# A chunked delta rule: chunk sums over halves of 64 tokens instead of 128 tokens

## The reference, cut to what matters

```python
def step(S, inp):
    r_t, w_t, k_t, v_t, kk_t, a_t = inp
    s_kk = jnp.einsum('bhij,bhj->bhi', S, kk_t)
    S = S * w_t[:, :, None, :] - s_kk[..., None] * (kk_t * a_t)[:, :, None, :] + v_t[..., None] * k_t[:, :, None, :]
    return S, jnp.einsum('bhij,bhj->bhi', S, r_t)
```

## Time and profile before

| | |
|---|---|
| time, median of 3 runs | 2954.65 us (2952.22 to 2955.24) |
| time of the profiled execution | 2943.12 us |
| its span | 2941.3 us |
| mean granted TensorE clock | 0.961 of 2.4 GHz |
| PE busy in the span | 2727.4 us (93%) |
| DVE busy | 991.0 us (34%) |
| ACT busy | 622.2 us (21%) |

### The profile page before, as it was taken

How to read it: one execution, slowest core, us unless ns; L and a number is a source line. 1 busy time by engine, 2 the same in 40 slices (tenths; PEclk the granted TensorE clock), 3 DMA queues, 4 the chain that set the end, 5 groups by cost and what they waited for, 6 DMA issues and landing times. The chain is left out here.

```text
span 2941.3 us, 35988 instructions
## 1 busy us (share of the span) xinstructions
PE 2727.4 (93%) x15314; PEld 1573.6 (53%) x15314; DVE 991.0 (34%) x2175; ACT 622.2 (21%) x1297; POOL 63.4 (2%) x61
## 2 busy tenths in 40 slices
PE   8998879899999989899679999999798986999998
PEld 7776645588874456574333333333585743444443
DVE  3513445223330238385611111111573752111212
ACT  4222215211110111272401000000313621000102
POOL 0000000000000000000001111111000000000000
PEclk9999979999999999999889999999898998999999
DMA  4137671122222031100369999999120027999995
GB/s 156 65 116 284 231 312 37 72 72 79 79 86 88 0 141 44 43 2 29 143 248 371 385 384 387 381 390 392 52 72 29 16 104 295 404 422 422 422 422 238
DMA packets 87476, 582.00 MB, mean 198 GB/s; under 512 B 10186, under 2 KB 11754, under 8 KB 21780
## 3 DMA queue, kind: packets, MB, share of 16 engines
q1 hardware_dynamic: 78244, 554.66, 47.9%
q0 software_dynamic: 6544, 21.24, 2.5%
q10 hardware_dynamic: 2528, 3.80, 0.3%
HBM read 561.96 MB, written 17.70 MB: 197 GB/s over the span
## 5 line engine op out<-in xcount | busy, mean ns | idle before, releaser
L1998 PE MATMUL ps<-both,ring 128*128 128x257 f32 x1408 | 308.6, 381 | 1.6 <-PEq L1628 1.6
L2911 PE MATMUL ps<-ring,xsL 128*64 128x512 f32 x1320 | 297.5, 602 | 5.7 <-ACTq L217 5.7
L1998 PEld LDWEIGHTS ps<-both,ring 128*128 128x128 f32 x1408 | 268.2, 191 | 42.0 <-issue 1.9
L2911 PEld LDWEIGHTS ps<-ring,xsL 128*64 128x64 f32 x1320 | 100.7, 139 | 193.7 <-issue 187.7
L3142 DVE TENSOR_TENSOR hidL<-hidL,ps 128x1024 f32<-128x1024 f32 x16 | 19.5, 1222 | 463.7 <-PE ps L2911 463.7
L1816 PE MATMUL ps<-ring,actT 128*128 128x512 f32 x352 | 153.6, 598 | 6.9 <-PEq L1986 6.9
L2510 PE MATMUL ps<-both,ring 128*128 128x384 f32 x480 | 157.5, 490 | 1.9 <-PEq L1809 1.9
L2911 PE MATMUL ps<-ring,htL 128*64 128x512 f32 x640 | 145.2, 605 | 3.4 <-ACTq L217 3.2
L856 PE MATMUL ps<-both,ring 128*128 128x264 f32 x640 | 143.8, 386 | 1.5 <-PEq L633 1.5
L3172 ACT ACTIVATE hidL<-ps 128x1024 f32<-128x1024 f32 x16 | 16.4, 1024 | 555.2 <-PE ps L2919 318.5
L856 PEld LDWEIGHTS ps<-both,ring 128*128 128x128 f32 x640 | 121.4, 190 | 23.0 <-issue 2.4
(11 more groups left out here) (536 smaller groups left out, 3671.6 us busy)
## 6 DMA issues: line engine op xcount, KB each, us to landing
ring<-in_w_exp SPq DMA_DIRECT2D x245, 1024.0 KB, 12.9
ring<-in_w SPq DMA_DIRECT2D x73, 1024.0 KB, 5.1
tokens_b<-in_w_exp SPq DMA_DIRECT2D x63, 1024.0 KB, 12.4
ring<-in_w_mod SPq DMA_DIRECT2D x48, 1024.0 KB, 5.2
h<-in_w_exp SPq DMA_DIRECT2D x37, 1024.0 KB, 17.1
lent<-in_w_exp SPq DMA_DIRECT2D x26, 1024.0 KB, 15.5
both<-in_w_exp SPq DMA_DIRECT2D x13, 1024.0 KB, 18.1
gb<-in_rows SPq DMA_DIRECT2D x8, 512.0 KB
```

The lines of the kernel that those rows point to most:

```text
L1998: mm = pe.matmul(k.ps[:, 4 * (j % 2) + 2 * gv + h, 0:HALF], w(c_), hT[:, c_, FIRST + h * HALF:FIRST + (h + 1) * HALF], start=c_ == 0, stop ...
L2911: mm = pe.matmul(ps[HD * par:HD * par + HD, bank + half, :], lhsL(kk, par), weights(kk)[:, half, par, :], start=kk == 0, stop=kk == KD - 1 ...
```

## The change

In step 10 the contraction is cut in two. The 128 tokens are taken as two halves (r = 0, 1) of 64 tokens; each half is contracted by itself, with 4 chunks x 64 = 256 moving columns, and goes to a PSUM bank of its own (bank + r), with g now choosing the left or right 256 columns of it. So there are 24 matmuls with a 64 x 64 stationary operand and 256 columns, in place of 12 with 128 x 64 and 512. They are also issued in another order: the two p and the two r of one product follow each other.

Since the halves are apart, one mask of four columns serves both: `side` is 1 where the token's chunk number modulo 4 is the column. So `ex` has four copies of each kind in place of eight: DVE makes four in step 9 in place of eight, ACT eight in `expand` in place of sixteen.

The diagonal of decays is written to `aT` by `keep_decay`, which DVE runs after it has announced step 9 (`steps.tell(moved.sem)`), and no longer in step 10. In step 10 DVE first waits for its own earlier instructions (`steps.join()`), then does the two subtractions. Reads of PSUM in step 10 now span two banks each.

For the tile of 16 tokens there is one half and one mask column, so its matmuls are the same 12 in another order.

```diff
--- before.py
+++ after.py
@@ -101,7 +101,7 @@
     parts["mask_u"] = np.concatenate([-1.0 * upper, 1.0 * upper], 1)
     parts["mask_o"] = np.concatenate([-1.0 * upper_in, 1.0 * upper_in], 1)
     parts["mask_l"] = -1.0 * lower
-    parts["chunk_of"] = (p[:, None] // CH == np.arange(CPT)[None, :])
+    parts["side"] = (p[:, None] // CH % 4 == np.arange(4)[None, :])
     parts["eye_head"] = (p[:, None] % HD == np.arange(HD)[None, :])
     parts["scan_keep"] = np.broadcast_to(np.arange(T1) % CH != 0, (P, T1))
     first_only = len(parts)
@@ -1167,8 +1167,9 @@
     tkn = sb("tok", [P, 4, RW])
     w = sb("tk", [P, 3, RW])
     spare = k.stream.ring[:, RING // 2:RING, :].rearrange("p s c -> p (s c)")
-    n_ex, n_a = 3 * CPT * RW, 2 * 2 * CPT * HD
-    ex = spare[:, 0:n_ex].rearrange("p (a c h) -> p a c h", a=3, c=CPT)
+    n_ex, n_a = 3 * 4 * RW, 2 * 2 * CPT * HD
+    ex = spare[:, 0:n_ex].rearrange("p (a c h) -> p a c h", a=3, c=4)
+    FOUR = 4 * CH
     aT = spare[:, n_ex:n_ex + n_a].rearrange("p (n g c j) -> p n g c j", n=2, g=2, c=CPT)
     gT = sb("gT", [P, 2, 2, P])
     hT_ = sb("hT_", [P, 2, 2, P])
@@ -1183,6 +1184,7 @@
     def steps_of(t):
         n, it = ns[t], t % 2
         nc_ = n // CH
+        groups, sides = -(-n // FOUR), min(nc_, 4)
         ts = slice(P * t, P * t + n)
 
         def hp(x, g, p):
@@ -1293,34 +1295,43 @@
 
         def dv9(dve):
             return [dve.tensor_tensor(gT[:, it, :, 0:n], both_g(0), rho[:, :, ts], ALU.add)] + [
-                dve.tensor_scalar(ex[0:n, 2, ch, :], w[0:n, 1, :], c("chunk_of")[0:n, ch:ch + 1], -1.0, ALU.mult, ALU.mult)
-                for ch in range(nc_)]
+                dve.tensor_scalar(ex[0:n, 2, x, :], w[0:n, 1, :], c("side")[0:n, x:x + 1], -1.0, ALU.mult, ALU.mult)
+                for x in range(sides)]
         out.append((pe9, dv9, lambda act: [act.copy(hT_[:, it, :, 0:n], both_g(1))]))
 
 
         def pe10(pe):
+            wide = sides * HD
             for g in range(2):
-                for p in range(2):
-                    s = head_cols(p, g)
-                    o = ps[HD * p:HD * p + HD, g, 0:nc_ * HD]
-                    pe.matmul(o, w[0:n, 0, s], ex[0:n, 0, 0:nc_, s], start=True, stop=True, skip_group_check=True)
-                    o = ps[HD * p:HD * p + HD, 2 + g, 0:nc_ * HD]
-                    pe.matmul(o, tkn[0:n, 2, s], ex[0:n, 1, 0:nc_, s], start=True, stop=False, skip_group_check=True)
-                    mm = pe.matmul(o, tkn[0:n, 1, s], ex[0:n, 2, 0:nc_, s], start=False, stop=True, skip_group_check=True)
+                for lhs, kind, bank, start, stop in ((w[:, 0], 0, 0, True, True), (tkn[:, 2], 1, 2, True, False),
+                                                   (tkn[:, 1], 2, 2, False, True)):
+                    for p in range(2):
+                        s = head_cols(p, g)
+                        for r in range(groups):
+                            b = slice(FOUR * r, min(FOUR * r + FOUR, n))
+                            mm = pe.matmul(ps[HD * p:HD * p + HD, bank + r, 256 * g:256 * g + wide], lhs[b, s], ex[b, kind, 0:sides, s],
+                                           start=start, stop=stop, skip_group_check=True)
             return mm
 
-        by_chunk = lambda bank: ps[:, bank, 0:nc_ * HD].rearrange("p (c j) -> p c j", j=HD)
+        by_four = lambda bank, g: ps[:, bank:bank + groups, 256 * g:256 * g + sides * HD]
+        fours_of = lambda x: x.rearrange("p (r c) j -> p r (c j)", c=sides)
 
         def dv10(dve):
             steps = k.v_steps
+            steps.join()
             for g in range(2):
-                d_ = Wend[:, g, CPT * t:CPT * t + nc_].unsqueeze(2).to_broadcast([P, nc_, HD])
-                e_ = c("eye_head").unsqueeze(1).to_broadcast([P, nc_, HD])
-                steps(dve.tensor_tensor(aT[:, it, g, 0:nc_, :], d_, e_, ALU.mult))
-                steps.free(dve.tensor_tensor(aT[:, it, g, 0:nc_, :], aT[:, it, g, 0:nc_, :], by_chunk(g), ALU.subtract))
+                a_ = fours_of(aT[:, it, g, 0:nc_, :])
+                steps.free(dve.tensor_tensor(a_, a_, by_four(0, g), ALU.subtract))
             return []
-        out.append((pe10, dv10, lambda act: [act.copy(fT[:, it, g, 0:nc_, :], by_chunk(2 + g)) for g in range(2)]))
+        out.append((pe10, dv10, lambda act: [act.copy(fours_of(fT[:, it, g, 0:nc_, :]), by_four(2, g)) for g in range(2)]))
         return out
+
+    def keep_decay(dve, steps, t):
+        nc_ = ns[t] // CH
+        e_ = c("eye_head").unsqueeze(1).to_broadcast([P, nc_, HD])
+        for g in range(2):
+            d_ = Wend[:, g, CPT * t:CPT * t + nc_].unsqueeze(2).to_broadcast([P, nc_, HD])
+            steps.free(dve.tensor_tensor(aT[:, t % 2, g, 0:nc_, :], d_, e_, ALU.mult))
 
     lists = [steps_of(t) for t in range(NT)]
     S = len(lists[0])
@@ -1407,6 +1418,8 @@
                     for x in lists[t][s][1](dve):
                         steps.free(x)
                     steps.tell(moved.sem)
+                    if s == S - 2:
+                        keep_decay(dve, steps, t)
                 if i is not None:
                     u, ch = i // CPT, i % CPT
                     if i + 1 < NCH:
@@ -1435,8 +1448,8 @@
                     act.wait_ge(made.sem, made.of(at(t - 1, S - 1)))
                 act.wait_ge(moved.sem, moved.of(at(t, 0)))
                 for a, src in enumerate((tkn[0:n, 1, :], tkn[0:n, 3, :])):
-                    for ch in range(n // CH):
-                        steps.free(act.activation(ex[0:n, a, ch, :], src, ACT.Identity, scale=c("chunk_of")[0:n, ch:ch + 1]))
+                    for x in range(min(n // CH, 4)):
+                        steps.free(act.activation(ex[0:n, a, x, :], src, ACT.Identity, scale=c("side")[0:n, x:x + 1]))
                 steps.tell(widened.sem)
 
             act.wait_ge(stepped.sem, stepped.of(1))
```

## The result

The changed kernel takes 2922.72 us (median of 4 runs, 2919.86 to 2924.57) against 2954.94 us before: ratio 0.9901, 95% interval 0.9887 to 0.9915. The medians differ by 32.2 us; the ratio, which is not the quotient of these medians, stands for 29 us (25 to 33). Forecast were 25 us and 2929.7 us. Two later sessions, with the kernel before measured beside it each time, gave 0.9909 (0.9886 to 0.9932) and 0.9902 (0.9887 to 0.9917), which is 27 and 29 us. The profiled execution took 2921.8 us.

What follows compares the result with a forecast made beforehand. DVE, PE and DVE end to end around step 10 were taken as the bound: 5.99 us a tile, four times 24.0, plus 0.75 and 0.2, about 25 us off 2954.65, giving 2929.7 us; own range 2925 to 2934, wide 2922 to 2941.

Steps and rivals of the forecast that it cites:

- What bounds the stretch: Step 9's DVE copies to the next tile's PE start: DVE, PE, DVE end to end, 11.91 us, four times.
- Copies: DVE's mask copies in step 9, four in place of eight: 1.05 us saved per tile.
- PE's step: PE's matmuls in step 10, four quadrants together: 2.78 us in place of 6.27, saving 3.49 us a tile.
- two quadrants at a time: Rival for PE's step 10: only two quadrants run at once, step 5.28 us, total 2940 us; chance 0.10.
- one after the other: Rival for PE's step 10: quadrants run in sequence, step 10.4 us, total 2961 us; chance 0.03.
- DVE in step 10: Two multiplications leave, two subtractions remain: 1.29 us in place of 2.74, saving 1.45 us a tile.
- Cover of the multiplications: Moved decay multiplications run on DVE while PE does step 10, costing nothing; uncovered, 1.29 us a tile.
- ACT: ACT's copies fall from sixteen to eight; nobody waits for them: 0 saved, at most 0.1 us per tile.
- the clock: Low-clock piece in the fourth tile's step 10, 1.50 us, may stay away: half counted, 0.75 us saved.
- The head and the last tile: Block up to the first tile's step 9: no saving counted; 16-token tile: 0.2 us saved, bounds 0.5 saved, 1.5 lost.
- A sign of being wrong: Stated in advance: the prediction is wrong if PE waits on DMA over a microsecond in the last tile.
- a saving given back: Rival: the weight stream paces the block and takes back the saving, time the same within 0.2%; chance 0.04.

Runs made afterwards that it cites:

- 3, halves: Kernel before with only the contraction over halves in four quadrants, masks and DVE's work as before: ratio 0.9961 (0.9947 to 0.9975).
- 4, multiplications: Kernel before with only the two decay multiplications moved behind the signal of step 9: ratio 0.9958 (0.9944 to 0.9973).
- 11: Changed kernel with the decay multiplications ahead of the signal for step 9, so PE waits for them: 2930.32 us, run once.
- experiment 7: Kernel before with step 10's twelve 128-token matmuls in the new order, p = 0 and 1 in turn: ratio 0.998 (0.997 to 0.9991).
- experiment 10: Changed kernel with ACT making sixteen copies a tile again, eight into space nobody reads: 2921.41 us, run once.
- 1, before again: Kernel before, unchanged, timed and profiled a second time: 2951.66 us median, ratio 0.9994 (0.998 to 1.0008); its block took 206.6 us.
- 2, changed kernel: Changed kernel, unchanged, timed and profiled again: 2926.44 us median, ratio to before 0.9909 (0.9886 to 0.9932).
- 8, changed kernel: Changed kernel once more, to compare with the early sums in the same session: 2920.65 us, ratio to before 0.9902 (0.9887 to 0.9917).
- 5, filled waits: Kernel before with unread matmuls added in PE's two waits around step 10: 2946.38 us median, ratio 0.9982 (0.9973 to 0.9991).
- 6, early sums: Changed kernel with F's first product ahead of step 9's wait, then A's with its own signal, F's second last: ratio to before 0.9901 (0.9886 to 0.9916).
- 12, early, filled: Early sums kernel with unread matmuls added in PE's wait after step 2 of each tile: 2916.05 us median, ratio to before 0.9879 (0.9861 to 0.9896).
- experiment 9: Changed kernel with step 10's passes ordered quadrant by quadrant, six passes of one, then the next: 2926.36 us, run once.

## Why the prediction was right, and which term was mis-sized

*What bounds the stretch:* right. DVE, PE, DVE end to end; each part shortened what was forecast (experiments 3, 4 and 11 each alone).

*Copies:* 1.05 forecast, 2.18 - 1.13 = 1.05 measured. *PE's step:* 2.78 us forecast, 2.82 measured, the modulation's matmuls being the right row to take it from. The rival of two quadrants at a time (5.28) and that of one after the other (10.4) are ruled out. Of the old 6.27 us, 0.90 was the order (experiment 7), and 2.5 the quadrants. *DVE in step 10:* 1.29 forecast and measured; reading two banks costs nothing. *Cover of the multiplications:* held; 1.20 us uncovered, 1.29 forecast. *ACT:* 0, as forecast (experiment 10).

*The sum of the four stretches:* 24.0 forecast. At full clock the four tiles went from 137.95 us (filled waits, same path) to 114.17: 23.8 us.

*The term that was mis-sized is the clock.* The prediction took it from the one low piece in the fourth tile, as half of 1.50 us, and took the first profile's block for a typical one. In the second profile of before the four tiles lose 144.32 - 137.95 = 6.4 us to the clock, in the first 1.5; all three profiles of the changed kernel have none. With it, the four tiles save 25.3 to 30.2 us. The first profiled execution was 11.5 us under its median, and the prediction called that "a matter of the whole run and not of this block". That was the wrong sentence: 9.0 of the 11.7 us between the two spans lie in this block.

One profile of a kernel is thin evidence, but every timed execution has its mean granted clock on record. At 1.2 GHz half of the time is lost at most (the 3.4 us of the fourth tile's piece cost 1.50 us), so (1 - mean clock) x span is an estimate of the loss, from above. Take its mean over all timed executions of a kernel, subtract it from that of the kernel before in the same session, and add what the stretch saves. The sum meets the measured gain within 3.5 us each time (all columns but the third in us):

| experiment | the stretch saves (trace) | clock, against before | clock gives (estimate) | sum | measured (ratio) |
|---|---|---|---|---|---|
| 1, before again | 0 | 0.9582, 0.9571 | 3.2 | 3.2 | 1.8 |
| 2, changed kernel | 23.8 | 0.9585, 0.9571 | 5.1 | 28.9 | 26.9 |
| 8, changed kernel | 23.8 | 0.9606, 0.9581 | 8.5 | 32.3 | 28.9 |
| 3, halves | 13.7 | 0.9567, 0.9571 | -0.6 | 13.1 | 11.5 |
| 4, multiplications | 5.8 | 0.9600, 0.9571 | 8.9 | 14.7 | 12.4 |
| 5, filled waits | 0 | 0.9600, 0.9581 | 5.7 | 5.7 | 5.3 |
| 6, early sums | 27.4 | 0.9585, 0.9581 | 2.3 | 29.7 | 29.2 |
| 7, order | 3.6 | 0.9588, 0.9581 | 2.2 | 5.8 | 5.9 |
| 12, early, filled | 27.4 | 0.9605, 0.9579 | 9.2 | 36.6 | 35.7 |

So what the stretch does not explain goes with the clock, each time. Experiment 5 shows that filling PE's two waits is enough to raise it. How much a wait costs cannot be counted from these runs: 3 and 7 both keep both waits and have -0.6 and 2.2 us, and in experiment 9 a low piece came without a long wait around step 10. Where the pieces fall stays open. The stretch itself was sized within 0.2 us. That the total came out only 2 to 7 us over the forecast is in part luck: the prediction counted 0.75 us for the clock, where the table has 5 to 9, and the head lost some. The measured median, 2922.72 us, lies below the prediction's own range of 2925 to 2934 and just inside the wide one, which starts at 2922.

*The head and the last tile* were forecast as 0 and 0.2 us. The head took 32.4 us in all three profiles of the changed kernel, 10.2 of them at 1.2 GHz, against 29.1 and 30.9 before: 1.5 to 3.3 us lost. Doubling ACT's copies did not bring it back (32.3 us), and the early sums had 30.4. Experiment 9, whose program is that of the changed kernel up to step 10 of the first tile, had 29.8, so the loss is not tied to the change; why is open. The last tile took 28.0 to 29.9 us against 29.1 and 31.4.

*A sign of being wrong that did show:* PE waiting on DMA for more than a microsecond in the last tile. It waited 1.06, 1.04 and 0.74 us in the three profiles. In the first of them PE idled 28.61 - 24.91 = 3.7 us in the last tile, at a clock of 1.00, where it had idled 29.05 - 27.25 = 1.8 us at 0.88:

```profile
384.71:413.76 29.05, 27.25 (x500) 17.80 (x500) 7.91 (x35) 3.34 (x12) 0.00 (x0) 0.88 0.90 362
```

So some of what the better clock gave there went into waiting, partly for the weights. The rival of a saving given back came true in this small part.

## What to carry to other kernels

Before a sum is set against a median, ask whether the profiled execution is typical; where it is faster or slower than the median, profile again and compare the granted clock in the block of the change, for a wait that a change removes can be worth more than its length. The mean clock of all timed executions tells it better than one profile. Independent small matmuls belong in turn into the quadrants of the array, row halves with a bank each (2.82 us in turn, 4.93 us in runs of six). Work of VectorE that needs no result of the coming step goes behind the signal that releases it.

## What the runs showed of the hardware that was not expected

- PE takes fp32 passes out of program order, but not freely: six in a row for one quadrant, eight times, took 4.93 us, the same 48 in turn 2.82.
- Matmuls that nobody reads, put into waits of 1.7 and 1.9 us, made a kernel 5.3 us faster (0.9982, 0.9973 to 0.9991), at a mean clock of 0.9600 against 0.9581.
- A gain of 3.6 us in four tiles (experiment 6) did not show in the time (0.9901 against 0.9902); in its profile the tile behind them ran at a clock of 0.76.
